# A conditioned decoder block on eight cores: GLA steps in another order, a bf16 gate product, work moved to GpSimd

## The reference

```python
mod = silu(c) @ w_ada + b_ada
shift1, scale1, gate1, shift2, scale2, gate2 = split(mod, 6)
h = rmsnorm(x, norm1_w) * (1 + scale1) + shift1
q, k, v, g, lr, cb, cc, cx, ga, gb = split(h @ w_in)
log_a = log_sigmoid(lr @ w_gate_up + b_gate) / 16
# gated linear attention: S_t = diag(a_t) S_{t-1} + k_t^T v_t ; o_t = q_t S_t
o = gla_chunked(q * 128**-0.5, k, v, log_a)
y_a = (rmsnorm(o, gla_norm_w) * silu(g)) @ w_proj_a
y_b = (cb * causal_conv3(cc * cx)) @ w_proj_b
z = sigmoid(ga) * y_a + sigmoid(gb) * y_b
x = x + gate1 * (z @ w_out)
h2 = rmsnorm(x, norm2_w) * (1 + scale2) + shift2
x = x + gate2 * (square(relu(h2 @ w_mlp1)) @ w_mlp2)
return rmsnorm(x, final_norm_w)
```

## Time and profile before

| | us |
|---|---|
| median of 3 runs | 1430.19 (1429.49 to 1430.9) |
| the profiled execution | 1430.64 |
| its span, slowest core (core 3) | 1428.9 |
| spans of the 8 cores | 1425.1 to 1428.9 |
| TensorE busy | 1304.3 (91%) |
| VectorE / ScalarE / GpSimd busy | 772.0 / 466.8 / 41.1 |

### The profile page before, as it was taken

One profiled execution on the slowest core, in us unless ns is written; L12 is line 12 of the kernel. 1 busy time (PEld: TensorE's weight loads), 2 busy tenths in 40 slices (PEclk: granted clock), 3 DMA queues, 4 the chain that ended last, 5 costly groups with the idle time before them and its releaser, 6 DMA issues.

```text
span 1428.9 us, 19232 instructions; the slowest of 8 cores (1425.1 to 1428.9 us)
## 1 busy us (share of the span) xinstructions
PE 1304.3 (91%) x6796; PEld 625.4 (44%) x6796; DVE 772.0 (54%) x1239; ACT 466.8 (33%) x1015; POOL 41.1 (3%) x72
## 2 busy tenths in 40 slices
PE   0498979898987999999999999999999999999996
PEld 0244355444443444444444444444444444444442
DVE  2366642467566555554332322667675565566678
ACT  2455542566543222233211111344302111211334
POOL 3000000000000000000000000000000000000001
PEclk9789989898998999999999999999999999999998
DMA  9933410100061154461131123700332031130212
GB/s 175 209 81 118 150 60 0 60 1 1 1 129 34 34 93 86 77 118 30 31 59 30 30 50 83 222 1 3 72 59 43 17 59 28 33 59 14 76 59 118
DMA packets 17981, 93.09 MB, mean 65 GB/s; under 512 B 2256, under 2 KB 2256, under 8 KB 12000
## 3 DMA queue, kind: packets, MB, share of 16 engines
q0 software_dynamic: 7632, 52.46, 20.6%
q1 hardware_dynamic: 10256, 39.40, 8.2%
HBM read 135.93 MB, written 8.39 MB: 101 GB/s over the span
## 4 chain that ended last, share of the span: by engine, by line
PE 80%; ACT 7%; DVE 5%; issue 4%; DMA 4%; DVEq 0%; ACTq 0%; SPq 0%
PE psf L266 78%; DMA xb<-x_prev 4%; ACT xn L239 2%; PE psf L276 2%; ACT tmp L239 2%; DVE tmp L242 1%; ACT on L239 1%; ACT S_bf L239 1%; DVE tmp L254 1%; DVE on L248 1%; DVE S L254 0%; ACT lnv L239 0%; DVE x L242 0%; DVE ub L242 0%; DVE ogT L257 0%
## 5 line engine op out<-in xcount | busy, mean ns | idle before, releaser
L266 PE MATMUL psf<-hT,wsl 128*128 128x512 bf16 x2944 | 668.4, 384 | 3.7 <-DVE cbuT L242 2.2
L266 PEld LDWEIGHTS psf<-hT,wsl 128*128 128x128 bf16 x2944 | 289.5, 99 | 352.8 <-issue 23.5
L239 ACT ACTIVATE tmp<-psf 128x512 f32<-128x512 f32 (+1 forms) x272 | 158.0, 584 | 601.2 <-PE psf L266 601.2
L266 PE MATMUL psf<-wsl,aT 128*128 128x512 bf16 x1024 | 223.3, 379 | 0.0
L242 DVE TENSOR_TENSOR aT<-tmp 128x512 bf16<-128x512 f32 x128 | 88.0, 692 | 120.6 <-ACT tmp L239 120.6
L266 PEld LDWEIGHTS psf<-wsl,aT 128*128 128x128 bf16 x1024 | 100.1, 98 | 120.6
L242 DVE TENSOR_TENSOR tmp<-tmp,psf 128x512 f32<-128x512 f32 (+1 forms) x72 | 45.2, 628 | 152.2 <-ACT tmp L239 152.2
L242 DVE TENSOR_TENSOR x<-x,tmp 128x512 f32<-128x512 f32 x160 | 116.4, 727 | 18.5 <-DVE tmp L242 3.6
L242 DVE TENSOR_TENSOR tmp<-psf,g2b 128x512 f32<-128x512 f32 x128 | 88.4, 690 | 26.7 <-PE psf L266 26.6
L254 DVE SCALAR_TENSOR_TENSOR tmp<-ub,cst,tmp 128x512 f32<-128x512 f32 x64 | 48.1, 751 | 35.5 <-ACT tmp L239 32.1
L266 PE MATMUL psf<-wsl,hT 128*128 128x512 bf16 x256 | 60.1, 379 | 4.0 <-ACT v L239 1.5
(11 more groups left out here) (147 smaller groups left out, 1072.1 us busy)
## 6 DMA issues: line engine op xcount, KB each, us to landing
wsl<-w POOLq DMA_DIRECT2D x16, 1024.0 KB, 9.6
wsl<-w_ada POOLq DMA_DIRECT2D x12, 1024.0 KB, 10.4
xb<-x_prev SPq DMA_DIRECT2D x16, 512.0 KB, 20.9
xb<-x_cur SPq DMA_DIRECT2D x16, 512.0 KB, 5.1
wsl<-w_merge POOLq DMA_DIRECT2D x8, 1024.0 KB, 8.2
x<-x_cur SPq DMA_DIRECT2D x16, 512.0 KB, 10.4
out<-x SPq DMA_DIRECT2D x15, 512.0 KB, 2.6
wsl<-w_conv POOLq DMA_DIRECT2D x8, 768.0 KB, 13.0
```

The source lines that it names most:

```text
L239: P.op("act", lambda e: e.activation(out=out, in_=in_, func=func, **kw), r, w)
L266: ins = e.matmul(out=o, lhsT=l, rhs=rh, start=st, stop=sp_)
```

## The change

1. **Gate product.** wg (16 rows, f32) becomes wg6 (128 rows, bf16): the weight is split into three bf16 parts, placed at rows 0, 16, 32, 48, 64 and 96 by six small DMAs from SP, and wlr is copied eight times side by side, so that the low-rank product has 128 rows. Its evacuation splits the product into bf16 parts as well, and each head's gate product is one bf16 matmul over 128 rows.
2. **Gate chain.** Exponential, Ln and scan work in place in Bt; Ln takes two heads at once; the two exponentials of Bt come behind every second head.
3. **Norms in pieces.** `norm` becomes `sq` (a Square; behind the fourth one Ln and Exp for all four) and `xscale` (on GpSimd, save in block 0). The pieces are put between others.
4. **Order.** Front: transposes of xn(0) stand ahead of `ada`, their evictions behind; norm(1) behind the gates of block 0. Blocks 1 to 3: transposes are woven with kprev; special_front stands in block 3. Loads of x(1), of q, v and the first conv weights and of the f32 q and k weights wait for named earlier loads.
5. **GpSimd** takes the casts of Mf, S_bf and x scalings.
6. **GLA.** The scaling into on is a piece of its own (phaseN), costs are new, the order is O(s), A(s+1), U(s+1), N(s), T(s), and dense(t) is ordered anew.
7. **Tail.** Output tiles 12 to 14 are scaled on VectorE like the others. `done_w` moves from `ada` to its callers.

```diff
-        wlr = sb("wlr", [128, 8, 16], BF16)
-        wg = sb("wg", [32, 512], F32)
+        wlr = sb("wlr", [128, 8, 128], BF16)
+        wg6 = sb("wg6", [128, 512], BF16)
...
+        for g in range(8):
+            Vcopy(wlr[:, :, g * 16:(g + 1) * 16], wlrs.t[:, :, :], wlrs.k(), ["wlr"])
...
+        Vcopy(part[0], wf, wgp[0][1], pk_[0])
+        Vtt(wr, wf, part[0], ALU.subtract, wgp[0][1] + pk_[0], wgp[3][1])
+        Vcopy(part[1], wr, wgp[3][1], pk_[1])
+        Vtt(part[2], wr, part[1], ALU.subtract, wgp[3][1] + pk_[1], pk_[2])
+        for n, (row, j) in enumerate(((0, 0), (16, 1), (32, 0), (48, 1), (64, 2), (96, 0))):
+            P.op("sp", lambda e, row=row, j=j: e.dma_start(out=wg6[row:row + 16, :], in_=part[j]), pk_[j] + ["wg6"],
+                 [("wg6", row)], dma=f"g{n}")
...
-        def norm(i):
...
+        def sq(i, s):
...
+            A(j_, xb.t[:, s, :], AF.Square, xb.k((s * 1024, 1024)), jk + [("ss", s)], accum_out=ss[:, s:s + 1])
+            if s == 3:
+                A(lnv[:, :], ss[:, :], AF.Ln, [("ss", s_) for s_ in range(4)], ["lnv"], scale=1.0 / D, bias=EPS)
+                A(rstd[:, :], lnv[:, :], AF.Exp, ["lnv"], ["rstd"], scale=-0.5)
...
+                Psmul(xn.t[:, s, :], xb.t[:, s, :], rstd[:, s:s + 1], xk + ["rstd"], xn.k((s * 1024, 1024)))
...
+                A(R, p_[:, :], AF.Copy, pk, lk)
+                Vtt(r_[:, :], p_[:, :], R, ALU.subtract, pk + lk, rk)
+                Vcopy(R[32:64, :], r_[32:64, :], rk, lk)
+                Vcopy(m_[96:128, :], r_[96:128, :], rk, lk)
+                Vtt(R[96:128, :], r_[96:128, :], m_[96:128, :], ALU.subtract, rk + lk, lk)
...
-                MM([(p_[:, :], wg[0:16, h * 128:(h + 1) * 128], lr_[0:16, :], True, True)], ["wg"] + lk, pk)
...
+                MM([(p_[:, :], wg6[:, h * 128:(h + 1) * 128], lr_, True, True)], WG + lk, pk)
...
+                A(Bt.t[:, h - 1:h + 1, :], Bt.t[:, h - 1:h + 1, :], AF.Ln, bk2, bk2, bias=1.0)
...
+        xload(1, after=[("w", 3)])
...
+            run([lr_piece(i + 1, ALLB), sq_piece(i + 2, 0), ms[0], ms[1], sq_piece(i + 2, 1), ms[2], ms[3]])
+            run([gs[0], gs[1], sq_piece(i + 2, 2), ms[4], gs[2], gs[3], sq_piece(i + 2, 3)] + ms[5:])
...
+                P.op("pool", lambda e, h=h: e.tensor_copy(out=Mb.t[:, h, :], in_=Mf.t[:, h, :]), Mf.k((h * 1024, 1024)),
...
-                            A(S_bf[(g + 1) % 2].t[:, h, :], S32.t[:, h, :], AF.Copy, S32.k((h * 256, 256)) + [("dec", par)],
...
+                            Psmul(S_bf[(g + 1) % 2].t[:, h, :], S32.t[:, h, :], dec[par][:, h * 4 + s:h * 4 + s + 1],
...
             out = [phaseA(0), phaseU(0)]
             for s in range(4):
...
+                out.append(phaseO(s))
+                if s < 3:
+                    out += [phaseA(s + 1), phaseU(s + 1)]
+                out += [phaseN(s), phaseT(s)]
...
-            if s < 12:
+            if s < 15:
                 late.append(whole)
```

## The result

The changed kernel takes 1467 us (1466.9 and 1467.9) against 1430.55 before: ratio **1.0259, interval 1.0234 to 1.0283, slower by 37 us**. The prediction was 1414, range 1393 to 1433. In two of the four executions, the profiled one among them, two cores of one die ran about 23 us longer than the others, so all rows of after are read on core 0, of the other die, with a span of 1464.2 us; before it was 1428.9.

The account below looks back on a forecast made before the run. Before 488 us TensorE waits and runs at a lowered clock, losing 71.5 us from 184 us on. Terms 5.5 + 21.7 - 13.9 - 7.1 - 19.3 - 3.2 = -16.3 take 1430.6 to 1414 us, range 1393 to 1433.

Parts of the forecast that it names:

- GpSimd's price: Cost of one 1024-column x scaling on GpSimd, taken as 1.1 us; the range keeps 2.35.
- GpSimd costs what its two-tensor row says: Rival, 0.18: scalings at 2.35 us add 20 us in blocks 1 to 4, S_bf chain adds 5: 1439 us, slower.
- The front: Start to the end of the low-rank product of block 1: +5.5 us, ending at 92.6 us.
- One turn: Loop between low-rank products, blocks 1 to 4: 36 us for 29.1, three times, +1 for special_front: +21.7 us.
- The term for the woven key products: In a loop turn, kprev 1 to 3 between the transposes that everyone waits for: 5.2 us.
- the loop is no longer than before: Rival, 0.20: one turn stays 29 us if ScalarE's waits are filled; the 21.7 go, 1393 us.
- To the first score product: From block 4's low-rank product: -13.9 us to the end of q and k, -7.1 in the rest of group 0.
- GLA groups and first conv pieces: S_bf off ScalarE and three dense groups covering the state update: -19.3 us of 46.2 lost in these stages.
- I put 2 us into those groups: GLA groups: 2 us charged for VectorE scans held beside GpSimd's scalings of x(6) and x(7).
- the GLA groups give nothing: Rival, 0.12: these groups are bound by VectorE and the scans at their start: +16, 1430 us, no change.
- The 3.5 us that the prediction left uncovered at each start: Each GLA group start: first intra product stands behind four scans (5 us), 3.5 of them uncovered.
- Tail: Three VectorE products replace three GpSimd ones, and ScalarE copies no longer precede the last Square: -3.2 us.

Follow-up runs that it names:

- e12: Changed kernel used to time GpSimd instruction forms, three x tiles not scaled properly: cast 1.03 us, two-tensor product with broadcast scale 1.88 us.
- e2: Changed kernel with only the S_bf scaling back on ScalarE, x still scaled on GpSimd: 1470.1 us, ratio 1.0271.
- e14: e13 with the S_bf scaling on ScalarE instead of GpSimd: 1402.8 us, ratio 0.9775.
- e1: Changed kernel with only the x scalings back on VectorE; S_bf and the Mb cast stay on GpSimd: 1439.8 us, ratio 1.0059.
- e7: e1 with the four key products of a block ahead of the next block's eight transposes, not woven between them: 1426.5 us, ratio 0.9972.
- e4: Kernel before, in its old order, with only x of blocks 1 to 7 and S_bf scaled on GpSimd: 1438.2 us, ratio 1.0047.
- e16: e13 with the gate product of blocks 6 and 7 in f32 as before: 1395.8 us, ratio 0.9725.
- e13: Changed kernel with low-rank weights loaded first, key products ahead of transposes, old GLA order, x of blocks 1 to 5 on VectorE: 1395.1 us, ratio 0.9715.
- e5: e1 with the old order and costs of the GLA pieces, normalisation inside the output piece: 1434.8 us, ratio 1.0024.
- e6: Kernel before with the new bf16 gate product alone: 1454.1 us, ratio 1.0162.
- e10: e7 with the old GLA order of e5 and a new front, low-rank weights loaded first and x(1) handled earlier: 1395.9 us, ratio 0.9749.
- e15: e13 with x of blocks 6 and 7 scaled on GpSimd by a two-tensor product with broadcast scale: 1396.5 us, ratio 0.9731.

## Why the prediction was wrong, by its own steps

**GpSimd's price, the step that failed.** "I take 1.1, near the memset, since there is one input to read instead of two." Measured 2.83. Neither end was a bound: the upper, 2.35, was another instruction, and e12 shows that on GpSimd a product of two tensors, one of them broadcast, can be quicker than a scaling. Put into the prediction's own sum, 6.9 us more in four places are +27.6: 1441.6. The stages of the ledger together came out 52 us above the prediction: these 27.6, 20 in the GLA stages below, and small differences elsewhere. The rival "GpSimd costs what its two-tensor row says", at 0.18, was thus the true mechanism with a price that was still too low; its threshold of 2.1 was passed. Its other half, that the S_bf chain adds 5 us, is refuted by e2 and e14. What the prediction quoted of the Trainium skill (GPSIMD Engine Reference, section 4.1, Engine selection), roughly line rate for one input, holds by these rows for the cast (1.03 us, about 1.0 ns a column) and not for the scaling; its other sentence, about twice as slow as VectorE, is too kind here, as VectorE took 0.79 in the mean for this tile before, 3.6 times less.

**The front (+15.8 for +5.5).** The first transposes (45.8 for 46.1) and the end of the first low-rank product (60.6 for 60) were right, the first partly by luck: wlr was there at 38.3 for 39.6, and its copies took 2.28 for 1.3. From there 42.3 us passed for 32.6. The first scaling began at 83.38, 22.8 us on, for 22.0 in the sum (16.8 to dP and 5.2 for the norm; the 92.6 comes out only with the evacuation of 3.2 inside the 16.8, as in a turn). GpSimd took 11.3 for 4.4, the price above. From the first transpose to the end of the product it was 8.1 for 6.2, all at a granted clock of 0.50: the product took 3.57 where the sum had 1.9. So of the 9.7 us, 6.9 are the price, 1.9 the cold restart, a term left out, and 0.8 came before the scaling. In e1, with x on VectorE, another wait shows: the reads of the key products stand behind the scalings of x(1) on VectorE, TensorE waits 11.68 us for kdT, and the stretch still takes 36.1.

**One turn (42.5, 43.6 and 42.7 us, the last with special_front, for 36 and +1).** 36 + 6.9 = 42.9, so the turn was right but for the price, as e1 shows by itself (34.7 to 35.3). The term for the woven key products, 5.2, measured 16.0 in three turns (e7), 5.3 each. So the prediction saw both costs of the loop, and the rival "the loop is no longer than before" was rightly kept low: it needs e7's order.

**To the first score product (-20.2 for -21.0).** Right in the sum. Its parts were 10 for 13.9 and 10.1 for 7.1: q and k took 40.8 us for 37, as q waited 2.34 us for Mf and restarted below full clock, and the rest was quicker.

**GLA groups and first conv pieces (+0.7 for -19.3), the second step that failed.** The prediction read 46 us of lost time in these stages as TensorE's to recover, and argued that three dense groups instead of two would cover the state. The runs split the 0.7 (stages 4 and 5 together, each a difference of two runs on their slowest cores):
- GpSimd's share in the old order -4.9 (e4 against before);
- the new list of dense groups, with Squares in pieces and the gate chain in pairs, -0.3 (e16, whose gates of these groups are f32, against e4);
- the bf16 gate product -4.1 (e13 against e16);
- the new order and costs of the GLA pieces +10.0 (after against e13), of which e5 shows 5.3 directly, with x on VectorE.

On the median core the same four are -7.2, +1.9, -4.8 and +11.4, so the second is none that can be told. The pairs also differ ahead of these stages, and the parts depend on their order: the gate product alone, in the old order, changed them by +0.7 (e6).

So the new order, which gave the prediction its third dense group, is what costs, and GpSimd's share, which the prediction charged with 2 us ("I put 2 us into those groups"), gives 5. The state was not what was late: TensorE never waits for S_bf in these groups, even at 3.62 us a step behind 12.23 us of x, and VectorE waits for it 1.4 us in four times. What is late is what VectorE and ScalarE owe a step in fixed order (`on`, `scb`, `ke`), and the new order asks for it sooner. The rival "the GLA groups give nothing" (0.12) named VectorE and the scans at the start of a group; that was the right engine. The 3.5 us that the prediction left uncovered at each start were near, with 3.88, 2.86 and 1.68.

VectorE was held beside GpSimd, though not to the end of GpSimd's instruction as in the earlier trace rows: in after two scans took 3.21 us, to 316.75, while GpSimd's second scaling ran on to 317.4. The two before them, of which GpSimd's scalings from 310.82 on met only the last part, took 2.34:

```profile
309.12 2.34 DVE L263 TENSOR_TENSOR_SCAN Bt<-smask,Bt 128x512 f32<-128x512 bf16 x2 [3.12 <-ACT Bt L239]
...
313.54 3.21 DVE L263 TENSOR_TENSOR_SCAN Bt<-smask,Bt 128x512 f32<-128x512 bf16 x2 [2.08 <-ACT Bt L239]
```

This is 0.9 us in each of two blocks, about the 2 us that the prediction put in, against 3.2 a block that VectorE no longer spends on x. With x on VectorE (e10) no scan there is longer than 1.23.

**Tail (-2.5 for -3.2).** Right: every last sum on VectorE is 0.69 us, the full-width product 1.28.

**Chances.** The cases with GpSimd cheap held 0.82, on an interpolation between a memset and a product that no row of a scaling supported. The range left out just the case that came, and no case held a GLA loss together with a dear GpSimd.

## What to carry to other kernels

Price an operation on GpSimd only from a row of the same instruction form; a cast, a product with a scalar and a product of two tensors differed by 1.03, 2.83 and 1.88 us for the same tile. Move work there only where nobody waits for the last of it: the same scaling cost 8 us a turn on a chain and gained 6 us in three groups beside dense TensorE work, as it cleared VectorE's queue. And the form that is quickest on GpSimd need not be the best: the one of 1.88 us held VectorE longer than the one of 2.83 and made the groups 5 us longer.

In an order written by hand, work that can run early belongs in front of the wait, not behind it (four key products, 16 us), and a transpose is asked for a step behind its normalisation, not at once (5 to 10 us here). And look at what the first instruction of each engine waits for: a load of 32 KB at the end of a queue of 4 MB set the first 45 us.

## What the runs showed of the hardware

- On GpSimd a 128x1024 scaling from f32 took 2.83 us with a scale per partition and 2.76 with a constant, 2.84 with f32 output; 256 columns took 0.92, 512 took 1.56 alone. A cast of the same tile took 1.03, a product with a broadcast tile 1.88.
- GpSimd and VectorE held each other. Beside GpSimd's scalings two scans took 3.21 us (e13), beside its product of two tensors 5.31 (e15), alone 2.34 (e10). The two of four scalings that overlapped scans took 3.3 us each, the other two 2.84, 12.23 together for 11.29 in the loop.
- With S_bf off ScalarE, ScalarE was busy for 48% instead of 57% of a stretch (69.52 us in 144.5, 88.70 in 155.1), and the stretch was 10.7 us shorter, though the engine was far from full in both.
- After waits of 7.46 us (e7) and 22.74 us (after) TensorE's granted clock was 0.50 in its next work: 32 transposes took 3.57 us, and a key product 3.23 for 1.89. Behind 3.32 us of waiting the same transposes took 3.03, at a mean clock of 0.61.
